# How far ScalarE rounds ahead of TensorE in the two down passes of a mixture-of-experts step: three quarters instead of five

## What is computed

```python
act = jax.nn.gelu(jnp.einsum('cd,chkd->chk', hc, expert_u[idx]))
return jnp.einsum('chk,chkd->cd', gate * act, expert_v[idx])
```

## Time and profile before

| | us |
|---|---|
| median of 3 runs | 2351.62 (2346.28 to 2355.62) |
| the profiled execution | 2334.83 |
| its span, first to last instruction | 2332.7 |
| first down pass, first L2197 to first L2221 | 1556.1 to 1928.7 |
| second down pass, first L2197 to its L2221 | 1940.12 to 2303.95 |

### The profile page before, as it was taken

One profiled execution on the slowest core, in us unless ns is written; L12 is line 12 of the kernel. 1 busy time (PEld: TensorE's weight loads), 2 busy tenths in 40 slices (PEclk: granted clock), 3 DMA queues, 4 the chain that ended last, 5 costly groups with the idle time before them and its releaser, 6 DMA issues. The chain is left out here.

```text
span 2332.7 us, 55190 instructions
## 1 busy us (share of the span) xinstructions
PE 2223.8 (95%) x16578; PEld 2144.1 (92%) x16578; DVE 1631.0 (70%) x2784; ACT 1202.5 (52%) x2217; POOL 735.9 (32%) x516
## 2 busy tenths in 40 slices
PE   9999999999999999999999999999888889888887
PEld 8999999999999999999999999999877778888886
DVE  8677788877767678888854445766666666666676
ACT  6445455556554445555554444455444444444453
POOL 0321100011010005888888882025432222122210
PEclk9999999999999999999999999999999998999998
DMA  7887666675556567878878887987777776777774
GB/s 237 284 291 244 200 206 206 205 251 183 186 178 201 162 184 185 188 181 187 179 168 208 184 185 209 318 249 243 252 265 260 265 267 215 253 246 254 241 256 144
DMA packets 337991, 514.35 MB, mean 220 GB/s; under 512 B 87276, under 2 KB 126564, under 8 KB 337772
## 3 DMA queue, kind: packets, MB, share of 16 engines
q1 hardware_dynamic: 263244, 427.59, 58.4%
q0 software_dynamic: 58016, 71.54, 12.3%
q10 hardware_dynamic: 16640, 14.16, 1.9%
HBM read 487.87 MB, written 25.24 MB: 220 GB/s over the span
## 5 line engine op out<-in xcount | busy, mean ns | idle before, releaser
L311 DVE TENSOR_TENSOR lo<-raw,hi 128x512 fp32r<-128x512 f32 x994 | 684.3, 696 | 361.3 <-ACT hi L306 340.3
L306 ACT CAST hi<-raw 128x512 fp32r<-128x512 f32 x996 | 608.8, 619 | 470.5 <-PE ps L327 444.4
L323 PE MATMUL ps<-h_hi,hi 128*128 128x264 f32 (+1 forms) x3200 | 822.4, 286 | 1.5 <-DVE h_lo L960 1.5
L324 PE MATMUL ps<-h_lo,hi 128*128 128x264 f32 (+1 forms) x3200 | 821.0, 286 | 0.0
L323 PEld LDWEIGHTS ps<-h_hi,hi 128*128 128x128 f32 x3200 | 602.5, 188 | 8.4 <-issue 5.7
L324 PEld LDWEIGHTS ps<-h_lo,hi 128*128 128x128 f32 x3200 | 602.8, 188 | 0.1
L327 PE MATMUL ps<-h_hi,lo 128*128 128x264 f32 (+1 forms) x3200 | 523.8, 285 | 6.3 <-DVE lo L311 6.3
L1732 POOL DMA_INDIRECT w_spill<-chosen,widx x256 | 440.7, 1721 | 268.0 <-DVE widx L1970 188.8
L327 PEld LDWEIGHTS ps<-h_hi,lo 128*128 128x128 f32 x3200 | 444.8, 188 | 8.4 <-DVE lo L311 8.4
L2201 PEld LDWEIGHTS ps<-whl,lo 128*128 128x128 f32 x2048 | 303.2, 191 | 113.4 <-DVE lo L2171 106.6
L2201 PE MATMUL ps<-whl,lo 128*128 128x216 f32 x2048 | 317.7, 278 | 77.2 <-DVE lo L2171 77.0
(11 more groups left out here) (309 smaller groups left out, 2142.7 us busy)
## 6 DMA issues: line engine op xcount, KB each, us to landing
raw<-u_tiles SPq DMA_DIRECT2D x512, 256.0 KB
raw<-expert_v SPq DMA_DIRECT2D x512, 256.0 KB
raw<-weights SPq DMA_DIRECT2D x480, 256.0 KB
w_spill<-zeros ACTq DMA_DIRECT2D x16, 864.0 KB, 6.0
wld<-w_spill SPq DMA_DIRECT2D x28, 432.0 KB, 4.5
qb<-q_spill POOLq DMA_DIRECT2D x8, 512.0 KB, 6.0
w_spill<-chosen,widx POOLq DMA_INDIRECT x256
u_spill<-ust SPq DMA_DIRECT2D x128, 24.0 KB
```

Of the source, the lines that this page charges most:

```text
L306: nc.scalar.copy(hi[k % SPLIT][:], raw_quarter(k)).then_inc(hi_done, 1)
L311: nc.vector.tensor_tensor(lo[k % SPLIT][:], raw_quarter(k), hi[k % SPLIT][:].bitcast(F32), ALU.subtract).then_inc(lo_done, 1)
L323: pe.matmul(out, a, rhs[0][:, first + j, 0:n], start=start and j == 0, stop=False)
L324: pe.matmul(out, a, rhs[1][:, first + j, 0:n], start=False, stop=False)
```

## The change

The constant FAR goes from 5 to the value of AHEAD, 3. Nothing else is edited.

```diff
     LATE = NK // 8 - 4
     FIRST = 4
-    FAR = 5
+    FAR = AHEAD
     LATE_ADDS = [(0, 2, 4, 6), (0, 2, 4, 6), (0, 2, 4, 6), (0, 2, 3, 4)]
```

## The result

The changed kernel takes 2282.45 us (median of 4 runs, 2280.2 to 2284.97) against 2353.62 for the kernel before (4 runs): 0.9697 of it, with a 95% interval of 0.9662 to 0.9732. That is 71 us saved. I had forecast 82 us, and a time of 2270 us.

What follows compares the result with a forecast made beforehand. The prediction took the down passes' loop through late loads and casts to the copy of W as the bound. Savings of 37 + 46 - 1 = 82 us gave 2270 us, range 2238 to 2325.

Steps and rivals of the forecast that it cites:

- The bound and the loop: Down passes: a loop over four chunks, from `lo` through loads and casts to the copy of W, sets the pace.
- First pass: First down pass: period falls from 6.02 to 5.25 us over 47.5 periods, saving 37 us.
- The reason with the rate: First pass: loads and gathers need 320 GB/s at 4.92 us a period, 300 at 5.25; 313 was carried before.
- The reason with the gathers: First pass: a 512 KB gather among the loads delays the r = 0 semaphore, which would fit the 8.10 us landing.
- Second pass: Second down pass: period falls from 5.78 to 5.05 us over 63 periods, saving 46 us.
- Less lead for the casts: Cast 2c+3 comes one step later; its loops of 8.4 and 9.3 us stay under 9.84, so cost nothing.
- Between the passes: Casts 3 and 4 of the second pass move behind four accumulator copies; at worst one cast, 0.6 us.
- The sum: Whole kernel: 37 + 46 - 1 = 82 us saved, taken unscaled from the median 2351.62, giving 2270 us.
- TensorE as the limit in both passes: Rival 1: r = 0 latency stays 5.9 us, nearly all 106 us come back, 2248 us; chance 0.16.
- Rival 2: Down passes: landing latency grows with the pace, periods 5.53 and 5.4 us, saving 47 us, 2305 us; chance 0.18.
- slower: Rival 4: the r = 1 cast loses a step of lead; at 12 us latency 46 us more, 2398 us; chance 0.06.
- Rival 3: Nothing gained: the copy of W is late for another reason, such as its wait for TensorE; 2352 us; chance 0.08.

Runs made afterwards that it cites:

- third run: The changed kernel, unedited and unpaced, on a third chip against the kernel before: 2282.61 us against 2357.3, ratio 0.9703.

## Why the prediction was right, and where it was off

**The bound and the loop.** Right. The loop from the subtraction through the loads to ScalarE's copy sets the period: three orders of the copy (FAR = 4, FAR = 3, between the casts) gave 5.79, 5.36 and 5.00 us in the first pass and 5.50, 5.05 and 4.93 in the second. I had said 5.83, 5.25 and 4.95, and 5.48, 5.05 and 4.92. For FAR = 4 that is the loop as summed; for FAR = 3 the two numbers were chosen near it.

**First pass: 37 us by the forecast, 31 us measured.** I took 5.25, about midway between the two latencies of the trace and near 300 GB/s. It is 5.36, since the late landing is the more frequent (29 of 39, as it was before with 34 of 44). With its median of 7.8 us the loop is 7.8 + 0.59 + 2.36 = 10.75 us, 5.38 a period. The reason with the rate was wrong: the same pass ran at 321 GB/s. The reason with the gathers was right: without them it is 4.87.

**Second pass: 46 us, and 46 us measured.** The number is right, and the way to it is not. I had the r = 0 cast at 5.93 us, TensorE as the limit at 4.92 with 0.8 us to spare in the loop, and 0.13 us on top for the first and last blocks. In fact the median landing went from 6.4 to 7.2 us, and the loop still sets the pace: 7.2 + 0.53 + 2.54 = 10.3 us at the median, 10.12 on average over the 61 loops that can be read, 5.06 a period. That my allowance was as large as this growth is luck.

**Less lead for the casts, costed at nothing.** Near enough: the copy ahead of both casts, a worse order than that of the change, cost some 6 us.

**Between the passes, costed at 1 us.** It cost nothing:

```profile
1937.18 1.23 DVE L2171 TENSOR_TENSOR lo<-raw,hi 128x1024 fp32r<-128x1024 f32 x1 [0.66 <-ACT hi L1787]
...
1938.80 0.60 PE L2201 MATMUL ps<-whl,lo 128*128 128x216 f32 x4
```

VectorE waits 0.66 us for the cast that was moved, its subtraction ends at 1938.41, and TensorE takes the result up at 1938.80 without a wait. The gap itself (7.8 us against 11.4 in the profiles on record, 11.4 against 7.6 when both are paced) follows the granted clock and not the kernel. TensorE is busy for all of it or all but 0.3 us, and the same 32 small products take 6.88 us of it in the kernel before, all at a granted clock of 0.50 to 0.61, and 3.77 in the changed one, at 0.98 from 1928 to 1931. At the low level the gap is 11.4 us in either kernel, and 6.5 in the changed one at 1.00 throughout (its third run).

**The sum.** It misses a term: the standstill at the start. It comes with the burst of small gathers. It is longer in the changed kernel, which had it in all three of its profiles: 114.2 - 80.5 = 34 us there, against 106.8 - 85.0 = 22 us in the one profile of before that has it, 12 us apart, and some executions of before are spared. (The paced runs in these differences are of the second chip; on one chip, with the copy between the casts, it is 114.3 - 80.6 = 34 us.) With pacing in both, the change is worth 2328.91 - 2246.66 = 82 us, of which the stages show 79: 31 and 43 us in the passes and 5 in the first 32 chunks, which I had left out. Without pacing it is 71. Taking the saving from the median without asking why the profiled execution was 17 us under it was the careless step: the standstill, which that execution was spared, is of this size.

**The rivals.** TensorE as the limit in both passes came, nearly, only with the copy between the casts, and wholly without the gathered rows. Rival 2, a latency that grows with the pace, is half right: in the first pass the landing stayed as it was; in the second its median grew from 6.4 to 7.2 us, where the rival had 7.7 and 5.4 a period. The time that rival 2 gave, 2305, did not come. Nothing, and slower: neither. Rival 3 used a formula that the Trainium skill, "DMA: Bandwidth & Descriptors", "Anatomy of one DMA", gives for DMAs that GpSimd issues; the quarters are loaded by SP, and 5.3 to 9 us passed from subtraction to r = 0 cast in the loops counted above.

## What to carry to other kernels

When a producer's small step waits in an in-order queue behind a step that waits for a load, ask which load it is, when that was issued, and what the loop back to its issue costs; here FAR from 5 to 4 was worth 0.2 to 0.3 us a period, from 4 to 3 0.4 to 0.5, and the copy between the casts another 0.4 and 0.1, until TensorE was the limit. The loop must be summed with the landing at the new pace, which was later in one of the passes. A delay that only shifts an engine's round is free until the round's end meets its deadline; it must not be added to the round. And a profiled execution that is well under the median of its own kernel is not the one to do sums against before the difference is explained.

## What the runs showed of the hardware that I had not expected

While GpSimd issues 32 indirect gathers of one column each nearly back to back (most take 0.95 us, with 0.3 us between them), ScalarE and VectorE start more than 30 us after the quarter that they wait for (1612.12 against 1578.4), although the timeline has its matmuls done; TensorE issues single matmuls some 2 us apart; and the DMA share falls to 0.13. The granted clock goes from 1.00 to its lower level, 0.50 or 1.2 GHz, between 1582 and 1584 us; TensorE had run without a pause before and had stood idle since 1579.2:

```profile
1580.00:1582.00 2.00, 0.00 (x0) 0.00 (x0) 0.00 (x0) 0.00 (x0) 1.69 (x2) 1.00 0.11 30
1582.00:1584.00 2.00, 0.00 (x0) 0.00 (x0) 0.00 (x0) 0.00 (x0) 1.39 (x3) 0.69 0.01 0
```

Spacing the same gathers by 1.7 us makes the standstill vanish, and starting them 19 us later moves it. Where it came, it cost 20 to 39 us an execution. The burst alone does not always bring it: the profile of before on record has the same 32 gathers, 1.60 us apart, and no standstill, and by the times of the kernel before it came hardly at all on one of the chips. What the burst holds up inside the chip stays open: no view shows it, and that it is TensorE's count that comes late is read from the waits, not seen.
